# The residual of a fused two-layer trunk: from transposes of x on TensorE to the stored normed x, and a narrow first block

## The chip, the cores and the metric

One core of a Trainium2 chip runs the whole kernel. The metric is device time in microseconds (us) of one launch, the median of three runs. Names of engines: PE is TensorE (PEld its weight loads), DVE is VectorE, ACT is ScalarE, POOL is GpSimd, SP is SyncE, which here only issues DMAs.

## The reference

Two layers over 256 latent and 256 context tokens of width 2048, all in float32. Layer 0 mixes tokens by neighbourhood attention, layer 1 by a state-space scan. Cut to what the change touches:

```python
mod = silu(c) @ ada_w + ada_b                 # shift, scale, gate for the latent tokens
mod_c = silu(c_ctx) @ ada_w + ada_b           # the same for the context tokens
h  = rms_norm(x, norm_w)   * (1 + scale)   + shift
hc = rms_norm(ctx, norm_w) * (1 + scale_c) + shift_c
y, yc = mixer(h, hc)                          # q, k, v, z = h @ w_in; 16 heads; (o * silu(z)) @ w_out
x   = x   + gate   * y                        # the residual of the output projection
ctx = ctx + gate_c * yc
```

Here rms_norm(x, w) is x divided by the root of its mean square (plus 1e-6), times w. The output is rms_norm(x, final_norm_w) after both layers.

## The kernel before

Everything is kept turned: features on the 128 partitions, the 512 tokens (256 latent, 256 context) in the free dimension, so a full activation is 16 feature tiles k of 128x512. A float32 product is made of three matmuls on rounded halves (hi*hi, lo*hi, hi*lo). One weight tile of 128 output columns is 1 MB, is split by ACT into w_hi (line 353) and by DVE into w_lo (line 357), and costs 48 matmuls in `project` (lines 373, 375, 377). Each engine's program is written out by hand, in order, with semaphores between engines. The parts that matter here:

**The first stage** (to 152 us). x is loaded, turned on PE (line 1963) and multiplied by one over its root mean square, which stands as a row repeated on all partitions in PSUM bank 3 (DVE, line 1303); the result is `xn_t`, 16 tiles. The modulation weights na_ada_w (shift and scale: 32 loads of 1 MB, n = 0 to 31) stream through four buffers. SP issues load n when `s_ada_used` says that load n-4 has been multiplied (`mod_products`, line 1995). `BLOCKS` lists which feature tiles are done together, as (first tile, number of tiles): the columns of a block must all be multiplied before any of its tiles has its scale and shift. A block of four tiles takes eight loads, in pieces of 2 KB, a block of two takes four loads, in pieces of 1 KB. When a block's loads are done, ACT copies the row sums (line 821), PE turns them into columns (`mod_columns`, line 2008), DVE adds the biases (lines 1312, 1316), and ACT, DVE and POOL make h (ACT line 796, DVE lines 1323 and 1345, POOL line 630). `first_tiles(c, p)` (lines 2022 to 2024) then multiplies half of a feature tile of block c by three of six weight tiles of the first heads, nine matmuls in one call; the six sums stay in six banks. Those weights come in eight loads of 0.79 MB (`load_first_weights`, line 421); `AHEAD` and `BEHIND` say in which block each stands. The order of `mod_products` and `first_tiles` on PE is the list at the end of the stage in the code.

**The first heads.** `first_heads` on ACT and DVE takes q, k, v, z of heads 0 and 1 from the banks (ACT lines 909 to 915), while `load_head` on SP brings the next weight tiles. Beside the heads the rest of na_ada_w and later ssd_ada_w (gate, and layer 1's modulation) is summed without PE: eight parts l = 0 to 7 in each head, each loaded by POOL (`load_ada`, line 605) into one of two buffers when DVE and ACT have read part l-2, multiplied by DVE (`ada_part`, lines 1409 and 1415) and ACT (`products`, line 858), and added by POOL (`add_products`, line 620).

**The output projection** (912 to 1076 us). 16 tiles of w_out. Behind the matmuls of tile m DVE computes x_t[m] = bank * gate + x_old (line 1555). x_old comes from x and ctx in DRAM: SP loads 128 columns of all tokens in two DMAs (line 471, pieces of 512 B), PE turns them by four transposes (`residual`, line 2169, called at k = 8 of each tile), ACT copies the bank to x_old (lines 968 and 1001). ACT then squares x_t[m] (line 971) and POOL adds the squares (line 693).

The arena is one SBUF buffer that the stages share by offsets. `xn_t` occupies 72 to 104 KB of it, and from the first head on q, k, v, the probabilities, the bias and the sums `ada_acc` and `ada_prod` lie in the same place.

## Time and profile before

| | us |
|---|---|
| median of 3 runs | 2076.57 (2076.32 to 2077.63) |
| the profiled execution, whole | 2077.76 |
| its span | 2075.9 |
| PE busy | 2017.7 |
| DVE busy | 1459.5 |
| ACT busy | 967.6 |
| POOL busy | 665.7 |

The span runs from the first to the last instruction of the profiled execution; its whole time is 1.9 us more. Busy time counts what an engine executes; PE's matmuls overlap, so a mean duration of 363 to 370 ns stands beside a step of 0.23 us from one to the next. The share of a DMA row is the mean busy share of 16 DMA engines, and PEclk 1.00 is the full TensorE clock, 0.50 half of it.

### The profile page before, as it was taken

What the parts mean: (1) busy time and instruction counts of PE and PEld (TensorE: products, weight loads), DVE (VectorE), ACT (ScalarE), POOL (GpSimd) and SP (SyncE); (2) the same over time, 40 slices, a digit from 0 to 9 for tenths busy, and PEclk for the clock granted to TensorE, in tenths of its full rate; (3) what the DMA queues carried; (4) which work ended last, traced back from release to release, by engine and by line L of the source; (5) the groups of instructions that cost most, each with busy time, mean ns of one, the idle gap of its engine ahead of it and who ended that gap; (6) DMA issues with size and microseconds to landing.
All of it is one profiled execution on the core that took longest, in us unless ns stands there. A gap on an engine that the chain in (4) does not pass through costs nothing.

```text
span 2075.9 us, 31012 instructions
## 1 busy us (share of the span) xinstructions
PE 2017.7 (97%) x10458; PEld 1674.5 (81%) x10458; DVE 1459.5 (70%) x2076; ACT 967.6 (47%) x1398; POOL 665.7 (32%) x568
## 2 busy tenths in 40 slices
PE   5998999999999999999999999999999999999998
PEld 3567888888888888878878888888888888888886
DVE  5248777777777777774348877787878787777544
ACT  3244444455444544453355445445444544456443
POOL 1035666556565655635200111111112111110011
PEclk7999999999999999999999999999999999999999
DMA  9996667666666666656353554554554645556654
GB/s 352 338 261 140 168 177 184 174 173 168 172 174 178 178 171 173 164 141 172 102 152 98 149 147 125 144 147 125 143 149 114 167 116 147 138 148 199 226 184 153
DMA packets 422706, 349.23 MB, mean 168 GB/s; under 512 B 13600, under 2 KB 366464, under 8 KB 422016
## 3 DMA queue, kind: packets, MB, share of 16 engines
q1 hardware_dynamic: 397552, 273.43, 46.0%
q0 software_dynamic: 19968, 70.26, 14.1%
q10 hardware_dynamic: 5136, 4.89, 0.7%
q8 instruction: 28, 0.46, 0.1%
q14 instruction: 22, 0.18, 0.0%
HBM read 344.21 MB, written 4.33 MB: 168 GB/s over the span
## 4 chain that ended last, share of the span: by engine, by line
PE 82%; DVE 7%; DMA 4%; ACT 3%; issue 3%; POOL 1%; SPq 0%; DVEq 0%; POOLq 0%; ACTq 0%
PE bank L373 21%; PE bank L377 20%; PE bank L375 20%; DMA arena<-in_na_ada_w_dram 3%; PE bank L2303 3%; PE bank L2305 2%; PE bank L2304 2%; DVE w_lo L357 2%; PE bank L2241 1%; DVE arena L1647 1%; PE bank L2222 1%; PE bank L2107 1%; PE bank L1995 1%; PE bank L2022 1%; PE bank L2236 1%
## 5 line engine op out<-in xcount | busy, mean ns | idle before, releaser
L373 PE MATMUL bank<-act_hi,w_hi 128*128 128x512 f32 (+1 forms) x2448 | 906.0, 370 | 11.5 <-DVE w_lo L357 7.0
L377 PE MATMUL bank<-act_hi,w_lo 128*128 128x512 f32 (+1 forms) x2448 | 888.6, 363 | 0.0
L375 PE MATMUL bank<-act_lo,w_hi 128*128 128x512 f32 (+1 forms) x2448 | 888.0, 363 | 0.0
L357 DVE TENSOR_TENSOR w_lo<-arena,w_hi 128x2048 fp32r<-128x2048 f32 x184 | 435.2, 2365 | 210.8 <-ACT w_hi L353 147.9
L373 PEld LDWEIGHTS bank<-act_hi,w_hi 128*128 128x128 f32 x2448 | 462.7, 189 | 97.3 <-issue 14.4
L377 PEld LDWEIGHTS bank<-act_hi,w_lo 128*128 128x128 f32 x2448 | 462.5, 189 | 73.6
L375 PEld LDWEIGHTS bank<-act_lo,w_hi 128*128 128x128 f32 x2448 | 463.2, 189 | 68.8
L620 POOL TENSOR_TENSOR acc<-acc,arena 128x512 f32<-128x512 f32 x224 | 328.5, 1467 | 126.5 <-ACT arena L858 117.2
L353 ACT ACTIVATE w_hi<-arena 128x2048 fp32r<-128x2048 f32 x138 | 263.8, 1911 | 84.5 <-PE bank L2305 78.2
L1415 DVE SCALAR_TENSOR_TENSOR arena<-arena,cond_c 128x512 f32<-128x512 f32 x240 | 249.4, 1039 | 63.9 <-DMA arena<-in_ssd_ada_w_dram 37.6
L858 ACT ACTIVATE arena<-arena,cond_c 128x512 f32<-128x512 f32 x256 | 171.3, 720 | 261.1 <-POOL acc L620 151.0
L1647 DVE SCALAR_TENSOR_TENSOR arena<-arena,convc 128x512 f32<-128x512 f32 (+1 forms) x192 | 154.0, 802 | 105.6 <-ACT arena L1043 92.4
L728 POOL TENSOR_TENSOR arena<-arena 128x1024 f32<-128x1024 f32 x32 | 76.5, 2392 | 469.3 <-ACT arena L1059 439.9
L1059 ACT ACTIVATE arena<-arena 128x1024 f32<-128x1024 f32 x32 | 33.9, 1060 | 206.0 <-DVE arena L1699 206.0
L2303 PE MATMUL bank<-w_hi,act_hi 128*128 128x512 f32 x256 | 101.1, 395 | 1.9 <-DVE w_lo L357 1.9
L2305 PE MATMUL bank<-w_hi,act_lo 128*128 128x512 f32 x256 | 99.8, 390 | 0.0
L2304 PE MATMUL bank<-w_lo,act_hi 128*128 128x512 f32 x256 | 99.7, 389 | 0.0
L717 POOL TENSOR_SCALAR_AFFINE_SELECT arena<-arena 128x256 f32<-128x256 f32 (+1 forms) x32 | 21.9, 717 | 206.5 <-ACT arena L1172 206.5
L901 ACT ACTIVATE w_hi<-arena 128x2048 fp32r<-128x2048 f32 x43 | 82.0, 1908 | 0.0
L605 POOL DMA_DIRECT2D arena<-in_ssd_ada_w_dram x96 | 68.3, 712 | 33.5 <-DVE arena L1415 25.9
L1048 ACT ACTIVATE arena<-arena 128x512 f32<-128x512 f32 (+1 forms) x48 | 28.6, 597 | 101.4 <-DVE arena L1647 101.4
L1072 ACT ACTIVATE arena<-arena 128x256 f32<-128x256 f32 x128 | 54.3, 495 | 24.2 <-POOL arena L717 24.2
(253 smaller groups left out, 2157.8 us busy)
## 6 DMA issues: line engine op xcount, KB each, us to landing
arena<-in_ssd_w_in_dram SPq DMA_DIRECT2D x81, 1024.0 KB, 6.0
arena<-in_na_w_in_dram SPq DMA_DIRECT2D x58, 1024.0 KB, 7.3
arena<-in_ssd_ada_w_dram POOLq DMA_DIRECT2D x96, 512.0 KB, 4.1
arena<-in_na_ada_w_dram SPq DMA_DIRECT2D x64, 512.0 KB, 8.0
arena<-in_ssd_w_out_dram SPq DMA_DIRECT2D x32, 1024.0 KB, 5.1
arena<-in_na_ada_w_dram POOLq DMA_DIRECT2D x32, 512.0 KB, 4.2
arena<-in_na_w_out_dram SPq DMA_DIRECT2D x16, 1024.0 KB, 6.3
arena<-cs_scr SPq DMA_DIRECT2D x64, 256.0 KB, 5.5
```

Source lines behind the costliest of these rows:

```text
L353: nc.scalar.activation(w_hi[:, n0 % 2, :], raw[slot], ACT.Copy).then_inc(s_hi, 1)
L357: nc.vector.tensor_tensor(w_lo[:, n0 % 2, :], raw[slot], w_hi[:, n0 % 2, :].bitcast(F32), ALU.subtract).then_inc(s_lo, 1)
L373: nc.tensor.matmul(out[:, 0:cols], hi[:, w], act_hi3[:, k, 0:cols], start=(k == 0), stop=False)
L375: nc.tensor.matmul(out[:, 0:cols], hi[:, w], act_lo3[:, k, 0:cols], start=False, stop=False)
L377: mm = nc.tensor.matmul(out[:, 0:cols], lo[:, w], act_hi3[:, k, 0:cols], start=False, stop=(k == KT - 1))
L620: nc.gpsimd.tensor_tensor(acc[:, :], acc[:, :], prod[:, h, :], ALU.add).then_inc(s_gp, 1)
L858: m = nc.scalar.activation(prod[:, h, :], ada_buf[l % 2][:, h, :], ACT.Copy, scale=cond_c[:, k, 1:2])
L1415: m = nc.vector.scalar_tensor_tensor(ada_acc, ada_buf[l % 2][:, h, :], cond_c[:, k, 0:1], ada_acc, ALU.mult, ALU.add)
L1647: m = nc.vector.scalar_tensor_tensor(u, xp[:, 0:segs, k:k + LAT], col(48 + 48 * k), u, ALU.mult, ALU.add)
L2303: nc.tensor.matmul(b[:, :], hi, w_hi[:, n % 2, w], start=(k == 0), stop=False)
L2304: nc.tensor.matmul(b[:, :], hi, w_lo[:, n % 2, w], start=False, stop=False)
L2305: mm = nc.tensor.matmul(b[:, :], lo, w_hi[:, n % 2, w], start=False, stop=(k == IT - 1))
```

## The change

- The residual no longer turns x. After the load of weight tile 6 SP writes `xn_t` to DRAM (`xn_scr`, four DMAs of 1 MB). In the output projection SP loads tile m of it in one DMA of 256 KB, DVE multiplies it by `std_row` (128x512), the root mean square of each token, and uses the product as x_old. The transposes on PE and the copies on ACT are gone.
- `std_row` comes from bank 3: ACT copies it in block 0 to `std_first`, DVE takes the reciprocal, ACT copies that to its place behind the last block.
- What overwrites `xn_t` now waits for the four stores (`s_xsp` 64): on ACT `products(1)` and with it q, k, v of the first head; on POOL `load_bias`; on DVE `ada_part(0)` stands behind z's gate. `ada_part(2)` and `(3)`, `products(3)` and `load_ada(4)` and `(5)` stand earlier in the first heads than before. `load_ada(0)` and `(1)` of the gate stand behind POOL's last piece of h, no longer before its last two.
- `load_x` waits until DVE has made the tile before in the same buffer (`s_free`), no longer for the transposes. POOL's first clearing of `sq_sum`, which lies at another place, waits for the last head.
- `BLOCKS` becomes 2, 4, 4, 4, 2 tiles in place of 4, 4, 4, 2, 2, with `AHEAD`, `BEHIND` and PE's order changed to fit.

What stands in a row on SP at the first stage's begin, before and after. Line 432 (435 in the changed kernel) loads na_ada_w in two DMAs for each n, line 421 (424) the first heads' weights.

```order
L415 DMA plain<-in_ctx_dram 128x2048
L432 DMA arena<-in_na_ada_w_dram 128x2x512 x8
L421 DMA arena<-in_na_w_in_dram 128x2x256 x2
L421 DMA arena<-in_na_w_in_dram 128x2x128 x2
L432 DMA arena<-in_na_ada_w_dram 128x2x512 [waits ada_used]
```

```order
L418 DMA plain<-in_ctx_dram 128x2048
L435 DMA arena<-in_na_ada_w_dram 128x4x256 x4
L424 DMA arena<-in_na_w_in_dram 128x2x256 x2
L424 DMA arena<-in_na_w_in_dram 128x2x128 x2
L435 DMA arena<-in_na_ada_w_dram 128x4x256 x4
L435 DMA arena<-in_na_ada_w_dram 128x2x512 [waits ada_used]
```

The first weights moved ahead of loads 2 and 3; loads 0 to 3 have half as long pieces and are all of block 0.

The end of the same stage on SP:

```order
L432 DMA arena<-in_na_ada_w_dram 128x4x256
L421 DMA arena<-in_na_w_in_dram 128x2x256 [waits first_w_lo_ready]
L421 DMA arena<-in_na_w_in_dram 128x2x256
L421 DMA arena<-in_na_w_in_dram 128x2x128 x2
L449 DMA arena<-in_na_w_in_dram 128x16x128 [waits ada_used] x2
```

```order
L435 DMA arena<-in_na_ada_w_dram 128x4x256
L424 DMA arena<-in_na_w_in_dram 128x2x256 [waits first_w_lo_ready]
L424 DMA arena<-in_na_w_in_dram 128x2x256
L424 DMA arena<-in_na_w_in_dram 128x2x128 x2
L452 DMA arena<-in_na_w_in_dram 128x16x128 [waits ada_used]
L457 DMA xn_scr<-arena 128x2048 [waits x_normed]
L457 DMA xn_scr<-arena 128x2048 x3
L452 DMA arena<-in_na_w_in_dram 128x16x128 [waits ada_used]
```

The four stores stand between the loads of weight tiles 6 and 7.

DVE in the first heads, from the last w_lo of the first stage on (1409 and 1415 are parts of the sums, 1422 and 1428 in the changed kernel; 1459 and 1472 make q_lo; 1361 and 1374 begin the softmax):

```order
L357 TENSOR_TENSOR w_lo<-arena,w_hi 128x2048
L1409 TENSOR_SCALAR arena<-arena,cond_c 128x512
L1415 SCALAR_TENSOR_TENSOR arena<-arena,cond_c 128x512
L1459 SCALAR_TENSOR_TENSOR rounded<-bank,rounded 128x512
L1465 TENSOR_TENSOR rounded<-bank,rounded 128x512
L1498 SCALAR_TENSOR_TENSOR arena<-arena,bank 128x512
L1415 SCALAR_TENSOR_TENSOR arena<-arena,cond_c 128x512 x2
L1459 SCALAR_TENSOR_TENSOR rounded<-bank,rounded 128x512
L1465 TENSOR_TENSOR rounded<-bank,rounded 128x512
L1361 TENSOR_TENSOR bank<-bank,arena 128x256 x2
L1366 TENSOR_REDUCE small<-bank 128x1 x2
L1368 TENSOR_REDUCE small<-bank 128x2
```

```order
L360 TENSOR_TENSOR w_lo<-arena,w_hi 128x2048
L1472 SCALAR_TENSOR_TENSOR rounded<-bank,rounded 128x512
L1478 TENSOR_TENSOR rounded<-bank,rounded 128x512
L1510 SCALAR_TENSOR_TENSOR arena<-arena,bank 128x512
L1422 TENSOR_SCALAR arena<-arena,cond_c 128x512
L1428 SCALAR_TENSOR_TENSOR arena<-arena,cond_c 128x512 x3
L1472 SCALAR_TENSOR_TENSOR rounded<-bank,rounded 128x512
L1478 TENSOR_TENSOR rounded<-bank,rounded 128x512
L1374 TENSOR_TENSOR bank<-bank,arena 128x256 x2
L1379 TENSOR_REDUCE small<-bank 128x1 x2
L1381 TENSOR_REDUCE small<-bank 128x2
L1428 SCALAR_TENSOR_TENSOR arena<-arena,cond_c 128x512 x2
```

Part 0 moved from before q_lo to behind z's gate, part 2 from behind the softmax and the next w_lo to right behind the maxima.

The diff, cut to its core:

```diff
 PRE_AT = (0, 2, 4, 5, 1, 3)
-BLOCKS = ((0, 4), (4, 4), (8, 4), (12, 2), (14, 2))
+BLOCKS = ((0, 2), (2, 4), (6, 4), (10, 4), (14, 2))
 FIRST_K = [k0 for k0, _ in BLOCKS]
-ADA_USED = [2 * k0 if nk == 4 else 24 + 2 * (k0 - 12) for k0, nk in BLOCKS] + [32]
-AHEAD = (0, 2, 4, 6, None)
-BEHIND = (1, 3, 5, None, 7)
+ADA_USED = list(itertools.accumulate([0] + [2 * nk for _, nk in BLOCKS]))
+AHEAD = (0, 1, 3, 5, None)
+BEHIND = (None, 2, 4, 6, 7)
 N_OUT_A = 4 * HEADS
...
-        x_st = [region(16 + 2 * s, 4, P) for s in range(2)]
+        x_st = [region(16 + 2 * s, TOK) for s in range(2)]
+        std_first, std_row = region(70, TOK), region(28, TOK)
         gate_part = region(30, P)
-        x_old, sq_a = region(22, TOK), region(20, TOK)
+        sq_a = region(20, TOK)
         w_third = [region(kb, D, of=rounded) for kb in (40, 48)]
...
-        sq_sum = region(28, TOK)
+        sq_sum = region(22, TOK)
         w_c = [region(kb, D, of=rounded) for kb in (32, 40)]
...
-            load_head(Turn(), (2, 3))
+            load_head(Turn(), (2,))
+            sp.wait_ge(s_xn0, KT)
+            for k in range(0, KT, 4):
+                sp.dma_start(xn_scr[:, k:k + 4, :], xn_t[:, k:k + 4, :]).then_inc(s_xsp, 16)
+            load_head(Turn(), (3,))
             with sp.Fori(2, HEADS) as i:
...
                 if i is not None:
-                    sp.wait_ge(s_xt, i * 2 + (u - 1))
+                    sp.wait_ge(s_free[u], i * 1 + 2 * HEADS)
                 elif u == 0:
                     sp.wait_ge(s_s, HEADS)
+                    sp.wait_ge(s_xsp, 64)
                 apart()
                 m = u if i is None else i * 2 + u
-                for t, src in ((0, x2), (2, ctx2)):
-                    sp.dma_start(x_st[u][:, t:t + 2, :],
-                                 src.rearrange("(t p) d -> p t d", p=P)[:, :, bass.ds(m * P, P)])\
-                      .then_inc(s_xst[u], 16)
+                src = xn_scr[:, m, :] if i is None else \
+                    xn_scr[:, bass.ds(m, 1), :].rearrange("p a t -> p (a t)")
+                sp.dma_start(x_st[u], src).then_inc(s_xst[u], 16)
...
                     pool.wait_ge(s_mod, FIRST_K.index(k) + 1)
-                if k == KT - 2:
-                    load_ada(0, None, True)
-                    load_ada(1, None, True)
                 if k >= 3:
...
+            load_ada(0, None, True)
+            load_ada(1, None, True)
             pool.wait_ge(s_h, KT)
+            pool.wait_ge(s_xsp, 64)
             load_bias(None)
...
             add_products(2, None)
+            load_ada(4, None, True)
             load_bias(1)
-            load_ada(4, None, True)
             add_products(3, None)
+            load_ada(5, None, True)
             mask_bias(1)
-            load_ada(5, None, True)
             for l in range(4, 7):
...
             pool.wait_ge(s_lo, N_OUT_A)
+            pool.wait_ge(s_o, HEADS)
             nc.gpsimd.memset(sq_sum, 0.0).then_inc(s_acc, 1)
...
                     first_hi(AHEAD[c])
+                if c == 0:
+                    act.wait_ge(s_xn0, KT)
+                    nc.scalar.activation(std_first, bank[3][:, :], ACT.Copy)
                 act.wait_ge(s_ada_used, ADA_USED[c + 1])
...
                     first_hi(BEHIND[c])
+            step(nc.scalar.activation(std_row, std_first, ACT.Copy))
+            step.wait()
...
                 act.wait_ge(s_h, KT)
-                for l in range(2):
-                    products(l, Turn())
+                products(0, Turn())
+                act.wait_ge(s_xsp, 64)
+                products(1, Turn())
                 act.wait_ge(s_pre, 1)
...
                 exp_scores(Turn())
+                products(3, Turn())
                 turned_probs(Turn())
...
                 next_hi(4, Turn(base=4))
-                for l in range(3, 8):
+                for l in range(4, 8):
                     products(l, Turn())
...
                     split_hi(act, n + 1, t2, (u + 1) % 2, landed(n + 1, t2))
-                act.wait_ge(s_xt, t2.at(u + 1))
-                nc.scalar.activation(x_old, bank[4 + u][:, :], ACT.Copy).then_inc(s_xo, 1)
                 act.wait_ge(s_free[u], t2.half(n // 2 + 1))
...
             act.wait_ge(s_raw[1], landed(n, Turn()))
-            act.wait_ge(s_xt, KT)
-            nc.scalar.activation(x_old, bank[5][:, :], ACT.Copy).then_inc(s_xo, 1)
             act.wait_ge(s_used, n - 1)
...
                     first_lo(BEHIND[c])
+                if c == 0:
+                    nc.vector.reciprocal(std_first, std_first)
...
                 split_lo(dve, 6, none, 0)
-                ada_part(0, none)
                 query_low(bank[4], none)
...
                 nc.vector.scalar_tensor_tensor(z_g, z_th, 1.0, bank[7][:, :], ALU.add, ALU.mult).then_inc(s_free[1], 1)
+                ada_part(0, none)
                 ada_part(1, none)
...
                 softmax(none)
+                ada_part(2, none)
                 split_lo(dve, 7, none, 1)
...
                 v_low(none)
-                ada_part(2, none)
+                ada_part(3, none)
                 probs_low(none)
                 split_lo(dve, 8, none, 0)
-                for l in range(3, 6):
+                for l in range(4, 6):
                     ada_part(l, none)
...
                     split_lo(dve, n + 1, t2, (u + 1) % 2)
+                dve.wait_ge(s_xst[u], 16 if i is None else i * 16 + 16)
+                nc.vector.tensor_tensor(x_st[u], x_st[u], std_row, ALU.mult).then_inc(s_xo, 1)
                 dve.wait_ge(s_used, t2.at(n + 1))
...
                         dst, bank[u][:, cols], mod_a[:, 2, s, u:u + 1] if i is None else mod_a[:, 2, s, m],
-                        x_old[:, cols], ALU.mult, ALU.add)
+                        x_st[u][:, cols], ALU.mult, ALU.add)
                 mm.then_inc(s_free[u], 1)
...
-            for q in range(8):
-                mod_products(0, q)
-                if q == 2:
-                    norm_rows()
+            mod_products(0, 0)
+            mod_products(0, 1)
+            norm_rows()
+            mod_products(0, 2)
+            mod_products(0, 3)
             mod_columns(0)
-            for c in (1, 2):
+            first_tiles(0, 0)
+            first_tiles(0, 1)
+            mod_products(1, 0)
+            mod_products(1, 1)
+            first_tiles(0, 2)
+            for q in range(2, 8):
+                mod_products(1, q)
+            mod_columns(1)
+            first_tiles(0, 3)
+            for c in (2, 3):
                 for q in (0, 2, 4, 6):
...
                 first_tiles(c - 1, 7)
-            for q in range(2):
-                first_tiles(2, 2 * q)
-                first_tiles(2, 2 * q + 1)
-            mod_products(3, 0)
-            mod_products(3, 1)
-            for p in range(4, 6):
-                first_tiles(2, p)
-            mod_products(3, 2)
-            mod_products(3, 3)
-            first_tiles(2, 6)
-            mod_columns(3)
-            first_tiles(2, 7)
+            for p in range(3):
+                first_tiles(3, p)
             mod_products(4, 0)
             mod_products(4, 1)
-            first_tiles(3, 0)
+            for p in range(3, 5):
+                first_tiles(3, p)
             mod_products(4, 2)
             mod_products(4, 3)
-            first_tiles(3, 1)
+            first_tiles(3, 5)
             mod_columns(4)
-            for p in range(2, 4):
+            for p in range(6, 8):
                 first_tiles(3, p)
...
-            def residual(u, t2, i):
-                pe.wait_ge(s_xst[u], 32 if i is None else i * 32 + 32)
-                if i is not None:
-                    pe.wait_ge(s_xo, t2.at(u - 1))
-                for t in range(4):
-                    mm = nc.tensor.transpose(bank[4 + u][:, t * P:(t + 1) * P], x_st[u][:, t, :], ident[:, :])
-                mm.then_inc(s_xt, 1)
-
             for u in range(2):
-                residual(u, Turn(), None)
                 project(pe, N_OUT_A + u, Turn(), parts=o_ready, ks=range(KT - 1, KT))
...
                 for u in range(2):
-                    project(pe, N_OUT_A + u, t2, parts=lambda k, u=u: residual(u, t2, i) if k == 8 else None,
-                            tile=first if u == 0 else None)
+                    project(pe, N_OUT_A + u, t2, tile=first if u == 0 else None)
...
             with pe.Fori(2, 5) as i:
```

## Rows read from the trace of the kernel before

**Rows 1.** The page: PE's busy time, and the chain that ended last by engine.
```profile
PE 2017.7 (97%) x10458; PEld 1674.5 (81%) x10458; DVE 1459.5 (70%) x2076; ACT 967.6 (47%) x1398; POOL 665.7 (32%) x568
PE 82%; DVE 7%; DMA 4%; ACT 3%; issue 3%; POOL 1%; SPq 0%; DVEq 0%; POOLq 0%; ACTq 0%
```

**Rows 2.** Windows, output projection, PE alone: length, busy (count), PEclk, DMA share, GB/s.
```profile
940.00:1060.00 120.00, 120.00 (x557) 1.00 0.47 128
```

**Rows 3.** Chain of work in the output projection: start, length, what.
```profile
1036.06 0.44 PE bank L2169 x4
1036.50 0.23 PE bank L373
```

**Rows 4.** Timeline of DVE, output projection: start, length, instruction, idle before.
```profile
1042.33 0.88 DVE L1555 SCALAR_TENSOR_TENSOR arena<-bank,mod_a,arena 128x256 f32 x2 [3.27 <-PE bank L377]
...
1077.02 0.69 DVE L1586 TENSOR_TENSOR arena<-arena 128x512 f32<-128x512 f32 x1
```

**Rows 5.** Timeline of PE, first block.
```profile
33.69 1.94 PE L1995 MATMUL bank<-arena 128*32 128x512 f32 x8 [4.24 <-DMA arena<-in_na_ada_w_dram]
...
44.48 1.87 PE L2008 MATMUL bank<-sel_mod,arena 128*128 128x4 f32 x8 [0.72 <-ACT arena L821]
49.03 0.79 PE L2022 MATMUL bank<-act_hi,w_hi 128*128 128x512 f32 x1 [2.68 <-DVE act_lo L1345]
```

**Rows 6.** Timeline of DVE, normalising x.
```profile
28.56 8.88 DVE L1303 TENSOR_TENSOR arena<-bank,arena 128x2048 f32<-128x2048 f32 x4 [4.11 <-issue]
```

**Rows 7.** Timeline of SP: the first loads of na_ada_w behind block 1's first products.
```profile
56.59 1.91 SPq L432 DMA_DIRECT2D arena<-in_na_ada_w_dram  x4
```

**Rows 8.** Windows, first stage: length; PE, PEld, DVE, ACT, POOL busy; PEclk, DMA share, GB/s.
```profile
44.00:54.00 10.00, 6.83 (x20) 5.70 (x21) 6.39 (x15) 5.85 (x10) 3.44 (x4) 0.52 1.06 383
54.00:58.00 4.00, 4.00 (x26) 1.94 (x25) 0.27 (x1) 0.00 (x0) 0.00 (x0) 1.00 0.42 110
...
66.00:114.00 48.00, 45.38 (x251) 28.91 (x253) 15.10 (x31) 13.57 (x22) 7.13 (x8) 1.00 1.07 361
...
128.00:142.00 14.00, 11.56 (x84) 8.08 (x76) 4.55 (x12) 6.06 (x8) 4.48 (x6) 1.00 1.05 300
```

**Rows 9.** Timelines of PE, POOL and ACT, end of the first stage.
```profile
134.82 0.50 PE L2008 MATMUL bank<-sel_mod,arena 128*128 128x4 f32 x4
...
142.25 0.66 PE L2022 MATMUL bank<-act_hi,w_hi 128*128 128x512 f32 x1 [2.69 <-DVE w_lo L1328]
...
152.12 0.60 PE L2115 MATMUL bank<-ident,arena 128*128 128x128 f32 x4
...
136.30 1.62 POOL L605 DMA_DIRECT2D arena<-in_na_ada_w_dram  x2 [9.79 <-DVE gain_a L1316]
...
148.91 0.60 ACT L909 ACTIVATE rounded<-bank 128x512 fp32r<-128x512 f32 x1 [4.65 <-PE bank L2024]
```

**Rows 10.** Windows of PE alone: clock behind two long waits.
```profile
142.00:146.00 4.00, 3.75 (x10) 0.57 0.95 47
...
200.00:204.00 4.00, 4.00 (x16) 0.52 0.80 199
```

**Rows 11.** Page, DMA issues (KB, us to landing): POOL's loads, a store; then line 449's loads.
```profile
arena<-in_na_ada_w_dram POOLq DMA_DIRECT2D x32, 512.0 KB, 4.2
...
x_scr<-arena ACTq DMA_DIRECT2D x1, 2048.0 KB, 8.8
...
DMA to landing us min/median/max: 8.7/10.1/11.5
```

**Rows 12.** Timelines of DVE, POOL, ACT and PE, heads 1 and 2.
```profile
153.41 1.53 DVE L1415 SCALAR_TENSOR_TENSOR arena<-arena,cond_c 128x512 f32<-128x512 f32 x2
...
183.60 2.66 POOL L620 TENSOR_TENSOR acc<-acc,arena 128x512 f32<-128x512 f32 x2 [1.65 <-ACT arena L858]
...
190.21 1.34 ACT L858 ACTIVATE arena<-arena,cond_c 128x512 f32<-128x512 f32 x2 [3.49 <-DMA arena<-in_na_ada_w_dram]
...
199.13 1.97 PE L2092 MATMUL bank<-ident,arena 128*128 128x128 f32 x8 [5.54 <-DVE arena L1379]
```

More of the change, by code:

```diff
@@ L15 @@
+import itertools
 from contextlib import ExitStack, contextmanager
```

3 lines of the change are left out of this document (2 added, 1 removed).

## The prediction

> **What bounds the kernel now.** I read the page first: PE is busy for 2017.7 of 2075.9 us and takes 82% of the chain that ended last [rows 1]. So what is saved on another engine counts only where PE waits for it, and what is saved on PE counts whole where nothing else holds it. Second, the windows of the output projection: in 120 us PE has no idle time, the clock is full and the DMA engines are half used [rows 2]. There PE alone sets the pace. Third, the first stage. DMA runs at 383 GB/s from 44 to 54 us, while PE is busy for 6.8 of these 10; then it falls to 110 GB/s for 4 us, because nothing had been issued until 56.59; from 66 to 114 it is full again at 361 GB/s, and PE is busy for 45.4 of 48 us [rows 7, 8]. So DMA and PE are nearly level in this stage, with DMA the slower, and time that the DMA engines idle there comes back as a wait. Last, the early heads: PE waits once for 5.54 us, at 199.13, and comes back at half clock [rows 10, 12].
>
> **The output projection.** It loses 16 times four transposes. The chain shows them at 0.44 us for four, beside 0.23 us for a matmul [rows 3]. 16 x 0.44 = 7.0 us, all on the path [rows 2]. ACT loses its 16 copies, DVE gains 16 products of 128x512 in SBUF; the nearest row is 0.69 us [rows 4]. They stand before the wait for PE, where DVE idles 3.3 us in a tile [rows 4], and cost nothing; if that cover were gone, each would cost up to 0.7 us, 11 in all. The load of x needs the evacuation of the tile two before instead of its transposes, half a tile (5.5 us) later, and SP's next w_out load stands behind it. It is then issued some 13 us before ACT splits it, and 1 MB loads landed in 8.7 to 11.5 us while the queue was full [rows 11], so it stays hidden. POOL's clearing waits for the last head; POOL is busy for a third of the span [rows 1] and has nothing else to do between the last head and the first square: nothing. **Term: -7.0 us**, from 0 (another engine takes the pace) to -7.4.
>
> **The start.** Block 0 needs four loads in place of eight. They have landed by about 33 us, when the fifth of before had (33.69) [rows 5], so the block waits for the normalised x: DVE starts that at 28.56 and needs 8.9 us [rows 6]. The norm's matmuls stand one load earlier, about 1 us, so 36.5. Then the copy for `std_first` (0.6, as ACT's copy of a bank at 148.91, rows 9), the row copy (0.6 with its start), two columns (half of 1.87 at half clock), and 2.7 us to h [rows 5]: first tile at 41.5, where it was 49.03. That is 7.5 us earlier. DVE's reciprocal of 128x512 costs 0.7 us at the rate of rows 4; DVE is busy for 15 of 48 us in such blocks [rows 8], and nothing waits for it. The rate of a wide reciprocal is in no row here. The Trainium skill (VectorE: DVE Perf Modes, walkthrough of the 8-slice pipeline) says that a reciprocal repeats its divide eight times; by that it would be an estimated 5 us, and the sum would be the same, as DVE's idle time holds that too.
>
> **What the start costs later.** Load 8 can be issued only when `mod_products(1, 0)` is done, and PE reaches that behind 18 matmuls of block 0. PE comes from a wait at half clock (0.52 in 44 to 54, rows 8): ten matmuls at 0.43 us and eight at 0.23 are 6.2 us, the product 1.0, so 48.8. Issued until then are x (4.2 MB), the small inputs (0.3), 8 loads (8.4) and two sets of first weights (1.6): 14.5 MB. Before, 19.5 MB (12 loads, three sets) were through at 54.0. The 5.0 MB less are 13 us at 383 GB/s, so the queue is empty at 41 to 43. It runs again 1.7 us behind an issue (56.59 to about 58, rows 7, 8), at 50.5. DMA idles some 8 us there, in place of 4 us at 54 to 58 [rows 8].
>
> From 50.5 on 24 loads and six sets of weights are left, 29.9 MB, at 361 GB/s 82.8 us: through at 133.3. The same sum for before, 24.9 MB from 58, gives 127, and 130 with its two later gaps. So the debt is about 3 us. PE through the rest: load 27 has four loads and two sets behind it, 5.8 MB or 16 us, and lands at about 118; product 1.0, half a tile of block 2 2.3, column to h 3.6 (4.55 at half clock less half of 1.87, rows 5): 124.8. Then 54 matmuls and four products, 16.5 us: the last column at 141.3, where it was 134.82 [rows 9]. From there to the last block's first tile were 7.4 us, 1.6 of them POOL's two DMA issues ahead of its h [rows 9], which the change moves behind it: 5.9, so 147.2 for 142.25. The last 36 matmuls took 9.9 us until 152.12, since PE came from 2.7 us of waiting at clock 0.57 [rows 9, 10]; at full clock 8.3. The wait is now 1.7 us and I can't tell which clock it leaves: 155.5 or 157.1. **Term: +4 us** (155.5 less 152.1 is 3.4, the other 5.0). Bounds: with the early rate of 383 GB/s all through (78.1 us for 82.8) the debt is gone and the term 0; with 300 GB/s, as at 128 to 142 [rows 8], for the last third of the bytes (10 MB, 5.6 us more) it is about +8.
>
> **The stores.** They are issued behind weight tile 6, whose load waits for the product at about 132. That tile landed 8.7 us behind its issue [rows 11], so 140.8. 4.2 MB at 361 GB/s are 11.6 us; by the kernel's one store of such a size (2 MB in 8.8 us, rows 11) 17.6. They end at 152.4 or 158.4. ACT wants them 3.2 us before PE's end (148.91 of 152.12, rows 9), at 152.9, with 1.4 us of `products(1)` between. Three copies at 0.65 us a step bring q, k and v to 150.9 before, 1.2 us ahead of PE at 152.12 [rows 9]. So at 152.4 nothing is lost (152.4 + 1.4 - 152.9 is 0.9); at 158.4 it is 5.7 us. Queued behind ACT's wait are q, k, v, z and w_hi of tile 7; behind POOL's wait the bias, which needs 6 to 7 us and is due at the softmax, 5.7 us behind PE's end. **Term: +1.5 us**, nearer to the first, as the stores have pieces of 8 KB and the 2 MB store has 1 KB. The Trainium skill (DMA: Bandwidth & Descriptors, anatomy of one DMA) gives about 2 us plus the bytes at 436 GB/s, for GpSimd's queue. By that the estimate is 11.6 us, and 6.8 for the 2 MB store, whose row says 8.8: the measurement is slower than the rule, which is why I don't take zero.
>
> **The first heads.** DVE now has part 0 (1.5 us as [rows 12]) and part 2 (1.5) between z and head 1's probabilities, and exp waits on ACT for part 2's load, which POOL can issue only behind part 0. I work out 0.3 to 1 us for PE's next turn. **Term: +0.7**, 0 to 3. In exchange the parts run ahead. Before, the last products stood at 190.21 behind 3.49 us of waiting for load 7; z's tanh follows them on ACT at 191.45, and 7.7 us later, at 199.13, PE may go on [rows 12]. PE was ready at 193.6. Now `ada_part(3)` and `products(3)` stand before the turned probabilities. Chained by POOL's 2.7 us an add [rows 12] and 4.2 us a load [rows 11], load 5 is issued near 168.5, load 6 at 177, load 7 at 180.6, and products(7) start at 185.5 (times as if the stage before had not moved). Probabilities are then ready at 194.5, for PE at 194.0: 0.5 us of wait in place of 5.54, and no half clock, which cost 2 us of the next 4 [rows 10]. **Term: -6.5**, 0 to -7.6.
>
> **Sum.** -7.0 + 4 + 1.5 + 0.7 - 6.5 = -7.3 us. The profiled execution took 2077.76 (span 2075.9), the median is 2076.57, 1.2 less; I take the difference from the median: 2069.3 us.
>
> **Rivals.**
> A. The early start holds: DMA runs faster than 361 GB/s with so few gaps, and the 7.5 us of block 0 stay. For it: 383 GB/s early, and PE idle only 2.6 of 48 us at 66 to 114. Against: the same rows have the DMA full in that time. -7.0 - 7.5 + 0.7 - 6.5 = -20: 2056.
> B. The second head's wait stays, because load 7 still comes late (it stands on six adds and four loads in a chain, and each late one shifts the rest). -7.0 + 4 + 1.5 + 0.7 = -0.8: 2075.8.
> C. Slower. The stores are the wait: they go at the 2 MB store's rate and share the engines with POOL's 1 MB of gate loads (2.9 us), end at 161, and q comes 8.6 us late for PE; the bias loads, which moved 47 GB/s with all engines occupied [rows 10] while PE was in the first stage, now stand in the first head and hold POOL's chain, so the later wait stays. -7.0 + 5 + 8.6 + 0.7 = +7: 2084. It decides if the stores end over 8 us behind PE's need (beyond 161).
> D. The output projection keeps its time, since a tile's evacuation with DVE's product becomes the bound: -7.3 + 7.0: 2076.
>
> **Chances.** Forecast 0.62 (its own range 2065 to 2073.5), A 0.10, B 0.14, C 0.10, D 0.04. What can be told from no change here is 0.2%, 4.2 us: faster takes the forecast and A, 0.72; B and D are the same, 0.17 with a small rest; C is slower, 0.11. The range of 2061 to 2078 leaves out A and C.
>
> **What would show it.** The first tile on PE at 41 to 42; GB/s near zero for some us before 50; the turn of v (the first PE work behind the stage) at 155 to 158 in place of 152.12; the stores landing near 152; no wait over 2 us on PE near 200; a tile of the output projection in 10.9 us and PE without idle time there. I am wrong in the front if DMA doesn't run dry at 43, and in the heads if PE's wait for the second head's probabilities (line 2092) stays above 3 us.

## The result, and the profile after

| | us (median of runs) |
|---|---|
| before, same chip | 2077.84 (2076.32 to 2080.68, 6 runs) |
| changed | 2086.31 (2083.77 to 2088.65, 6 runs) |
| ratio changed / before | 1.004 (95%: 1.003 to 1.0051) |

The change makes the kernel 8.5 us slower here, and 6.5 us slower in a second series (r12 below). The forecast was 2069.3, and the range ended at 2078: it was wrong in sign. The profiled execution of after is its slowest, 2088.65 us with a span of 2087.0, so it stands 11.1 us behind the span of 2075.9 before. Page of the changed kernel, answering to [rows 1]:

```profile
PE 2015.1 (97%) x10394; PEld 1673.3 (80%) x10394; DVE 1492.3 (72%) x2093; ACT 957.0 (46%) x1384; POOL 693.2 (33%) x568
PE 52%; DMA 12%; DVE 11%; issue 11%; POOL 7%; ACT 6%; POOLq 0%; DVEq 0%; ACTq 0%; SPq 0%
```

PE has 2.6 us less to do, but it is only half of the chain that ended last, where it was 82%. That half belongs to this execution and not to the change: the page of r12, the same kernel, says 82% again, and r8, which is faster than before, has 51%. What these two executions share is told under r12.

The first stage, PE and then windows (columns as in [rows 8]), for [rows 5, 8, 9]. Line 2011 is now `mod_products`, 2024 `mod_columns`, 2038 the first matmul of `first_tiles`:

```profile
41.22 0.80 PE L2038 MATMUL bank<-act_hi,w_hi 128*128 128x512 f32 x1 [2.67 <-DVE act_lo L1356]
...
57.86 1.94 PE L2011 MATMUL bank<-arena 128*32 128x512 f32 x8 [1.59 <-DMA arena<-in_na_ada_w_dram]
60.74 1.93 PE L2011 MATMUL bank<-arena 128*32 128x512 f32 x8 [0.94 <-DMA arena<-in_na_ada_w_dram]
64.17 1.93 PE L2011 MATMUL bank<-arena 128*32 128x512 f32 x8 [1.50 <-DMA arena<-in_na_ada_w_dram]
...
121.38 1.07 PE L2011 MATMUL bank<-arena 128*32 128x512 f32 x8 [1.03 <-DMA arena<-in_na_ada_w_dram]
...
144.75 0.50 PE L2024 MATMUL bank<-sel_mod,arena 128*128 128x4 f32 x4
...
151.34 0.47 PE L2038 MATMUL bank<-act_hi,w_hi 128*128 128x512 f32 x1 [1.85 <-DVE w_lo L1339]
```

```profile
44.00:50.00 6.00, 6.00 (x29) 3.61 (x27) 3.24 (x2) 1.48 (x1) 0.00 (x0) 0.72 0.01 3
...
58.00:74.00 16.00, 12.85 (x45) 6.50 (x44) 4.29 (x14) 5.20 (x10) 3.57 (x4) 0.50 1.06 379
...
78.00:80.00 2.00, 2.00 (x18) 0.64 (x11) 0.00 (x0) 0.00 (x0) 0.00 (x0) 1.00 0.15 26
```

The first tile comes at 41.22, as forecast, and the DMA is dry from 44 to 50 (3 GB/s). When it runs again, PE takes each load as it lands, with waits between, and from 58 to 74 it has half the clock (0.50, the 1.2 GHz level). The last column ends up at 144.75 for 134.82 [rows 9]. (r12 has it at 143.49, after a first tile at 39.79: one execution of this kernel differs from another by over a microsecond here.)

The end of the stage and the first head: SP, POOL, ACT, then PE, for [rows 9, 12]. Line 457 issues the stores, 612 the gate's loads, 647 the bias, 871 is `products`, 923 takes q; on PE 2132 turns v, 2109 turns the probabilities:

```profile
136.16 5.48 SPq L457 DMA_DIRECT2D xn_scr<-arena  x4
...
147.19 1.61 POOL L612 DMA_DIRECT2D arena<-in_na_ada_w_dram  x2
153.93 1.33 POOL L647 DMA_DIRECT2D arena<-in_na_rpb_dram  x2 [5.13 <-DMA xn_scr<-arena]
...
159.52 1.33 ACT L871 ACTIVATE arena<-arena,cond_c 128x512 f32<-128x512 f32 x2 [7.65 <-DMA arena<-in_na_ada_w_dram]
161.31 1.34 ACT L871 ACTIVATE arena<-arena,cond_c 128x512 f32<-128x512 f32 x2 [0.46 <-DMA arena<-in_na_ada_w_dram]
162.55 0.57 ACT L923 ACTIVATE rounded<-bank 128x512 fp32r<-128x512 f32 x1
```

```profile
164.15 1.12 PE L2132 MATMUL bank<-ident,arena 128*128 128x128 f32 x4 [4.38 <-ACT arena L927]
183.61 1.79 PE L2109 MATMUL bank<-ident,arena 128*128 128x128 f32 x8 [3.01 <-DVE arena L1392]
...
213.81 1.09 PE L2109 MATMUL bank<-ident,arena 128*128 128x128 f32 x8 [0.55 <-DVE arena L1392]
```

Read the first block from the bottom. q (162.55) stands behind two pairs of gate products on ACT, and these wait for POOL's loads issued from 147.19 on, which land at 159.5 and 161.3. That is 12.2 and 13.1 us for 0.5 MB each, where the page of before has 4.2 as the median [rows 11] and 5.3 to 5.7 for these two. The stores themselves were through at 153.9 at the latest (POOL goes on there), 6 us before PE's last first tile ended. So the wait for the stores, which I had priced, costs nothing, and the loads that share the engines with them cost 4.38 us on PE.

The 11.1 us, read from the start of the same instruction in both traces ("turned probabilities" is PE's transposition of them, line 2092 before and 2109 now):

| PE reaches | before | after | later by |
|---|---|---|---|
| end of first tiles | 152.12 | 159.77 | 7.6 |
| turn of v | 152.12 | 164.15 | 12.0 |
| turned probabilities, head 0 | 165.61 | 183.61 | 18.0 |
| the same, head 1 | 199.13 | 213.81 | 14.7 |
| the same, head 3 and on | 301.82 | 314.81 | 13.0 |
| the same, last head | 897.65 | 914.50 | 16.9 |
| span's end | 2075.9 | 2087.0 | 11.1 |

### The profile page after: what moved, and what is told of

Read it like the earlier page. It is cut to its first block, busy times and chain, and to the rows that moved or that the text cites. A ratio compares the mean times of both kernels' runs of the same rounds, so it can differ in the third digit from the quotient of the medians.

```text
span 2087.0 us, 30856 instructions
## 1 busy us (share of the span) xinstructions
PE 2015.1 (97%) x10394; PEld 1673.3 (80%) x10394; DVE 1492.3 (72%) x2093; ACT 957.0 (46%) x1384; POOL 693.2 (33%) x568
## 3 DMA queue, kind: packets, MB, share of 16 engines
q0 software_dynamic: 19968, 70.26, 13.5%
## 4 chain that ended last, share of the span: by engine, by line
PE 52%; DMA 12%; DVE 11%; issue 11%; POOL 7%; ACT 6%; POOLq 0%; DVEq 0%; ACTq 0%; SPq 0%
PE bank L376 12%; PE bank L380 12%; PE bank L378 12%; DMA arena<-in_ssd_ada_w_dram 7%; POOL acc L627 4%; DMA arena<-in_na_ada_w_dram 4%; ACT arena L871 3%; PE bank L2310 3%; PE bank L2312 2%; PE bank L2311 2%; DVE arena L1428 2%; DVE w_lo L360 2%; POOL acc L621 2%; PE bank L2248 1%; DVE arena L1663 1%
## 5 line engine op out<-in xcount | busy, mean ns | idle before, releaser
L360 DVE TENSOR_TENSOR w_lo<-arena,w_hi 128x2048 fp32r<-128x2048 f32 x184 | 443.9, 2412 | 193.3 <-ACT w_hi L356 150.3
L627 POOL TENSOR_TENSOR acc<-acc,arena 128x512 f32<-128x512 f32 x224 | 335.9, 1499 | 136.3 <-ACT arena L871 127.1
```

Source lines behind the costliest of these rows:

```text
L360: nc.vector.tensor_tensor(w_lo[:, n0 % 2, :], raw[slot], w_hi[:, n0 % 2, :].bitcast(F32), ALU.subtract).then_inc(s_lo, 1)
L627: nc.gpsimd.tensor_tensor(acc[:, :], acc[:, :], prod[:, h, :], ALU.add).then_inc(s_gp, 1)
```

## The experiments

The ratios are to runs of the kernel before in the same series, "r1" and so on name the kernels. The change stands at 2086.31 in its own series and at 2083.91 in r12's, 2084.6 over all eleven executions, which lie between 2082.89 and 2088.65. So where a variant of the change is set beside it, a difference of 2 to 3 us or less can't be told from none, and the traces have to speak.

**r1, the residual alone** (with PE's order of before for these blocks).
```
-BLOCKS = ((0, 2), (2, 4), (6, 4), (10, 4), (14, 2))
+BLOCKS = ((0, 4), (4, 4), (8, 4), (12, 2), (14, 2))
-AHEAD = (0, 1, 3, 5, None)
-BEHIND = (None, 2, 4, 6, 7)
+AHEAD = (0, 2, 4, 6, None)
+BEHIND = (1, 3, 5, None, 7)
```


> The changed kernel with the blocks of before put back (4, 4, 4, 2, 2 columns, with their loads and their order on TensorE); the residual from the stored normed tokens stays. Theory A (the narrow first block runs the DMA dry at 44 to 50 us and makes all that follows late, the gate's first loads above all; the residual's part is a gain): the stage of the first tiles ends at 152 to 153 us as before, the out projection is 6 us shorter, the waits of the first heads stay under 4 us in all: 2070 to 2075 us. Theory B (it is the stores of 4 MB and the order of the first heads that cost): the turn of v still comes 5 us or more behind the last first tile, and the time is over 2080.

2074.73 us, ratio 0.9986 (0.9977 to 0.9995).

**r2, the blocks alone**, the kernel before with the new table and PE's new order:

> The kernel before with nothing but the new blocks (2, 4, 4, 4, 2), their loads and their order on TensorE. Theory A: the first stage ends at 158 to 160 us instead of 152.1, the DMA is dry from 44 to 50 us, and the second head's wait near 200 us stays: 2082 to 2087 us, as slow as the full change or slower. Theory B: the front costs little, 2076 to 2080.

2086.95 us, ratio 1.0047 (1.0034 to 1.0061). So the blocks alone cost 9.3 us, and the residual alone wins 2.9. The two add up to 6.4 us, beside the 8.5 and 6.5 of the change. PE in r1:

```profile
151.58 0.66 PE L2131 MATMUL bank<-ident,arena 128*128 128x128 f32 x4 [2.14 <-ACT arena L927]
170.76 1.97 PE L2108 MATMUL bank<-ident,arena 128*128 128x128 f32 x8 [5.50 <-DVE arena L1392]
...
200.93 1.09 PE L2108 MATMUL bank<-ident,arena 128*128 128x128 f32 x8
```

The time is in theory A's range, but its "waits under 4 us in all" fails: the first head still waits 7.6 us. And the stage of the first tiles ends at 149.4, not at 152 to 153, mostly by the clock. The last 36 matmuls stand behind a wait of 1.85 us in r1 and took 8.4 us at full clock; r6 has the same blocks and the same wait, was granted 0.61 over the next 4 us, and needs 9.9. r2 has the last column at 142.47 and no wait at the turn of v (159.76) or at the first probabilities (173.26): 7.6 us later than before at both. Its second head waits 5.10 us, where before waited 5.54.

**r3, two products ahead of the first tiles.**
```
+            mod_products(1, 0)
+            mod_products(1, 1)
             first_tiles(0, 0)
             first_tiles(0, 1)
-            mod_products(1, 0)
-            mod_products(1, 1)
```


> The changed kernel with the second block's first two groups of modulation products ahead of the first tiles on TensorE, instead of behind two of them. Theory A: the loads behind them are issued at about 40 us instead of 49.5, the DMA does not run dry, TensorE does not wait at 55 to 66 us and keeps its full clock there; the last column comes at 138 to 140 us instead of 144.9, the stage ends 4 to 6 us earlier, and the time is 2079 to 2082 us. Rival: the transfers are only moved, another gap takes the place of this one, and less than 2 us are won (2085).

2080.51 us, ratio 1.002 (1.0011 to 1.0029): 5.8 us less than the change in its first series, 3.4 less than in r12's.

```profile
44.00:50.00 6.00, 6.00 (x34) 4.01 (x37) 3.05 (x2) 1.49 (x1) 0.00 (x0) 1.00 0.80 294
...
56.31 1.71 PE L2011 MATMUL bank<-arena 128*32 128x512 f32 x8 [3.99 <-DMA arena<-in_na_ada_w_dram]
59.03 1.94 PE L2011 MATMUL bank<-arena 128*32 128x512 f32 x8 [1.01 <-DMA arena<-in_na_ada_w_dram]
...
138.55 0.50 PE L2024 MATMUL bank<-sel_mod,arena 128*128 128x4 f32 x4
```

The dry stretch holds 294 GB/s now, and the last column is 6.2 us earlier. TensorE still waits for two loads (5.0 us), which A had denied, while the DMA moves 341 to 394 GB/s (56 to 68 us). And the last column is still 3.7 us later than before: filling the dry stretch wins back 6.2 of the 9.9 us by which the change is late there (144.75 for 134.82).

**r4, copies of q, k, v ahead of the gate's products on ACT.**
```
-                products(0, Turn())
                 act.wait_ge(s_xsp, 64)
-                products(1, Turn())
...
+                products(0, Turn())
+                products(1, Turn())
```


> The changed kernel with ScalarE's copies of the first head's q, k and v and its tanh ahead of the first two pairs of gate products, behind the wait for the stores. If q waits for the gate's first loads (landed at 159.5 and 161.3 us): the turn of v is no longer later than the last first tile by more than 2 us, 2.5 to 4 us are won there, and some 2.5 at the end (2083 to 2084). Rival: the chain of gate products, then 3 us later, sets the first head's probabilities or the second head, and nothing is won (2086).

2084.38 us, ratio 1.0032 (1.002 to 1.0044), between the two series of the change. The turn of v follows the last first tile without a wait (159.48). The first probabilities then wait 6.74 us:

```profile
179.87 1.97 PE L2109 MATMUL bank<-ident,arena 128*128 128x128 f32 x8 [6.74 <-DVE arena L1392]
...
210.44 1.09 PE L2109 MATMUL bank<-ident,arena 128*128 128x128 f32 x8 [0.85 <-DVE arena L1392]
```

4.7 us at the turn of v become 3.7 at the first head's probabilities, and 0.9 at head 2's (264.05 for 264.90): PE then waits 2.08 us for w_lo (at 237.95), for 1.18 in the change. So the first half of the expectation holds and the gain at the end does not; the rival was right that the chain of gate products takes it back.

**r5, the stores early**, ahead of the ninth load of the modulation (and no longer behind weight tile 6).
```
+                    for k in {8: (0, 4, 8, 12)}.get(n, ()):
+                        sp.wait_ge(s_xn0, KT)
+                        sp.dma_start(xn_scr[:, k:k + 4, :], xn_t[:, k:k + 4, :]).then_inc(s_xsp, 16)
                     if n >= 4:
                         sp.wait_ge(s_ada_used, n - 3)
```


> The changed kernel with the four stores of the normed tokens issued ahead of the ninth group of modulation weights (at about 39 us, into the stretch where the DMA is dry) instead of at 136 us. Theory A (the stores share the DMA with the gate's first loads and hold TensorE's first head): the gate's loads land within 7 us of their issue instead of 12 to 13, q does not wait for them, and the turn of v follows the last first tile within 1 us; the stores last some 10 us, of which 6 to 7 fill the dry stretch, so the last column is 0 to 3 us later: 2080 to 2084 us. Rival C (the stores are harmless, the wait comes from the late last column alone): the gate's loads still take over 10 us, 2086 to 2089.

2082.82 us, ratio 1.0027 (1.0016 to 1.0038): 3.5 us less than the change in its first series, 1.1 less than in r12's, so the time decides little. The 44 to 50 window moves 426 GB/s. POOL, ACT and PE:

```profile
148.57 1.61 POOL L612 DMA_DIRECT2D arena<-in_na_ada_w_dram  x2
...
153.26 2.63 ACT L871 ACTIVATE arena<-arena,cond_c 128x512 f32<-128x512 f32 x4
...
162.59 0.60 PE L2132 MATMUL bank<-ident,arena 128*128 128x128 f32 x4
```

The loads land 4.6 and 5.0 us behind their issue; ACT takes the gate's products and waits for neither. So the stores' share of the DMA was what made these loads late: the "harmless" of this expectation's rival C is refuted. The last column is 1.4 us later (146.13), as A had it, and the last 36 matmuls ran at half clock here (0.57 over their first 4 us), at full clock in the change. So the turn of v is only 1.6 us earlier, and of the 2.8 us at the first probabilities 0.7 are left at head 2's (264.21).

**r6, r1 with the first head's order of before** (r4's edit, and on DVE):
```
                 softmax(none)
-                ada_part(2, none)
                 split_lo(dve, 7, none, 1)
                 normalise(none)
                 v_low(none)
-                ada_part(3, none)
+                ada_part(2, none)
                 probs_low(none)
```


> The blocks of before with the stored residual (2074.7 us), and in the first head the order of before again: ScalarE's copies ahead of the first gate products, VectorE's third and fourth part behind the copy of v and the low half of the probabilities. In that kernel TensorE waited 2.14 us at the turn of v and 5.50 us at the first turned probabilities, at half clock behind it. Theory A (the order of the first head and the late gate loads cost together): the first wait goes, the second is under 3 us; but the second head's wait comes back in part, since part 2 and the fourth load are later: 2071 to 2074. Rival: the wait only moves to the second head, as the kernel before had it there (5.5 us), 2074 to 2077.

2075.35 us, ratio 0.9989 (0.998 to 0.9998): no gain over r1. The first probabilities are 1.6 us earlier than in r1 (169.13), those of the second head, behind a wait of 4.91, 2.7 later (203.62 for 200.93). The rival holds: a part taken out of the first head is missing in the second.

**r7, the change without DVE's product.** It leaves out the scaling of the normed x back to x.
```
-                nc.vector.tensor_tensor(x_st[u], x_st[u], std_row, ALU.mult).then_inc(s_xo, 1)
+                dve.sem_inc(s_xo, 1)
```


> The changed kernel without VectorE's product of the stored tokens with the factor in the out projection (the residual added there is the normed tokens, not scaled back: this part of the computation is left out). The product's price on TensorE's path is read off: TensorE waited 0.38 us at 932.1 and 1.29 us at 944.5 for VectorE. Theory A: 1 to 1.7 us, 2084.5 to 2085.5. Rival: 16 products by 0.68 to 1.79 us hold VectorE, and the port they share with GpSimd makes more of it: over 3 us, 2083 or less.

2085.27 us, ratio 1.0041 (1.0028 to 1.0055): 1.0 less than the change in its first series, 1.4 more than in r12's. The time shows no price of the sixteen products, and speaks against the rival's 3 us. In the trace the wait at the projection's third tile goes from 1.29 to 0.48, 0.8 us; the rest of that projection is alike.

**r8, r6 with two of the four stores early**, one ahead of load 12 of the modulation and one ahead of load 28:

> The kernel of r6 with one store ahead of the 13th group of modulation weights (about 47 us), one ahead of the 29th (about 106 us), and only two at 128 us. Theory A: each store of 1 MB costs 2.5 us of DMA, the first two fall into stretches where it had room (56 to 60 and 112 to 116 us); the gate's loads land by 144 us and the bias is there 5 us earlier; another 1 to 3 us against r6: 2069 to 2073. Rival: the DMA is the bound from 60 to 112 us, and the first store makes the stage 2.5 us later: as r6 or slower.

2073.1 us, ratio 0.9979 (0.997 to 0.9988). It is 2.3 under r6, with intervals that overlap. The first head waits 1.89 us for r6's 3.32, the second 5.68 for 4.91:

```profile
201.53 1.97 PE L2109 MATMUL bank<-ident,arena 128*128 128x128 f32 x8 [5.68 <-DVE arena L1394]
```

**r9, r1 with four stores spread**, and DVE's first part ahead of the copies again:
```
+                    for k in {12: (0,), 18: (4,), 24: (8,), 28: (12,)}.get(n, ()):
+                        sp.wait_ge(s_xn0, KT)
+                        sp.dma_start(xn_scr[:, k:k + 4, :], xn_t[:, k:k + 4, :]).then_inc(s_xsp, 16)
...
                 split_lo(dve, 6, none, 0)
+                ada_part(0, none)
                 query_low(bank[4], none)
```


> The blocks of before, the stored residual, and its four stores ahead of the 13th, 19th, 25th and 29th group of modulation weights; VectorE's first part ahead of the copies of q and k again, its third part ahead of the normalisation as in the change. Theory A (late gate loads behind the stores, and parts that VectorE then does between softmax and normalisation, are what the residual's part paid in the first head): the gate's first loads land within 6 us of 137, the turn of v comes at 152, the first turned probabilities at 168 or before (170.8 in the kernel with the late stores), the second head has no wait over 1 us; with the out projection 2069 to 2072 us. Rival: four early stores take 10 us of DMA in a stretch that is bound by it, the last column is 3 us or more later: 2073 to 2077.

2072.44 us, ratio 0.9979 (0.997 to 0.9988).

```profile
168.33 1.09 PE L2108 MATMUL bank<-ident,arena 128*128 128x128 f32 x8 [1.65 <-DVE arena L1392]
197.00 1.09 PE L2108 MATMUL bank<-ident,arena 128*128 128x128 f32 x8 [0.70 <-DVE arena L1392]
```

Both waits are small at last. The time is just over theory A's 2069 to 2072. The rival has its part: there are four waits for loads between 69 and 135, where before had two, and the last column is 138.18 for 134.82, 3.4 later. r9 changes two things, the stores' place and part 0's, and no run separates them. A wait that before did not have is left: 2.31 us for w_lo at 224.75, with DVE's w_lo behind ACT's w_hi, and that behind gate products which waited 3.19 us for POOL's add. r8, r9 and r10 can't be told apart in time; they are the fastest, some 4 to 5 us (0.2%) under before and 11 to 14 under the change.

**r10, r9 with tile 1's product beside tile 0's:**

> The same, with the product for the out projection's second tile done beside that of the first, ahead of the sums of the gate, instead of between the gate's first part and the evacuation of the tile. Theory: the evacuation of tile 1 is 0.7 to 1.1 us earlier, TensorE's wait of 1.3 to 1.7 us at tile 3 shrinks to 0.5, and the time is 1 us less than without it, at the edge of what these runs can tell. Rival: the load of tile 3 sets that wait, no difference.

2072.56 us, ratio 0.9975 (0.9965 to 0.9985). The wait at the third tile shrinks as expected, 1.66 to 0.48. The medians are 0.1 us apart and can't show a microsecond, and between the two profiles the first stage differs by 3.6 us in its end, 1.6 of them by the clock behind the same wait of 1.85 us. Inconclusive in time, clear in the trace.

**r11, the new blocks with everything mended** (r3's and r9's edits on the change):

> The new blocks (2, 4, 4, 4, 2) with the two groups of products ahead of the first tiles, and the stores and VectorE's first part as in the two kernels before this. Theory A (first tiles 8 us earlier buy nothing, since the stage is bound by the loads to 112 us and TensorE does the same work): 2 to 5 us slower than the same with the blocks of before, 2073 to 2076. Rival (the new blocks are a gain once nothing holds them): as fast or faster, 2070 or less.

2075.54 us, ratio 0.999 (0.9978 to 1.0003), 3.1 more than r9. A holds, though the intervals of r9 and r11 overlap: the first tile is 6.4 us earlier (42.07 for 48.50), the turn of v 6.2 us later (159.20 for 153.03). PE waits for loads six times between 56 and 121.

**r12, the change again:**

> The changed kernel again, with nothing altered. In its profiled execution (2088.65 us, its slowest) the chain of gate products ran 4 us later within each head than in that without the product, and TensorE lost 3.9 us more at the end of the heads. If that belongs to single executions: a profile without it (last turned probabilities 14.6 us behind the last turn of v, not 18.4) or a time near 2084 to 2085 beside others near 2088. If it belongs to the kernel: 18.4 us again.

2083.91 us (2082.89 to 2087.67), ratio 1.0035 (1.0021 to 1.0049). PE's waits in the last head, first the change, then this run:

```profile
900.94 0.47 PE L376 MATMUL bank<-act_hi,w_hi 128*128 128x512 f32 x1 [2.17 <-DVE act_lo L1534]
...
908.15 0.50 PE L376 MATMUL bank<-act_hi,w_hi 128*128 128x512 f32 x1 [1.91 <-DVE act_lo L1534]
```

```profile
903.58 0.50 PE L376 MATMUL bank<-act_hi,w_hi 128*128 128x512 f32 x1 [1.43 <-DVE act_lo L1534]
```

The 3.9 us at the end of the heads belong to single executions: the last probabilities stand 14.6 us behind the last turn of v here, as in before and in ten of the other kernels. The distance was 18.4 in that first profile and 17.3 in r8's. The chain of ACT, POOL and DVE over the gate's products goes with it. In r12 its last products on ACT begin 2.2 us behind the turn of v in heads 2 and 3, as in the first profile; at head 4 they are 1.3 us ahead of it, and from head 5 on 2.4. In the first profile they stay 1.5 to 2.6 us behind to the last head. r7 makes the same step at head 5. So there are two rhythms, and most executions leave the late one after a few heads; what makes them leave it stays open.

## Why the prediction was wrong

Three terms failed: what the start costs later, the stores and, by most, the first heads. By the prediction's terms, in the profiled execution (in brackets: forecast):

- **The start [first tile at 41.5]**: 41.22, and 39.79 in r12. Right, with some luck in the tenths, and so was the DMA's dry stretch [41 to 43, again at 50.5: the 44 to 50 window].
- **What the start costs later [+4, bounds 0 to +8]**: +7.6, and +7.6 in r2 alone. This is the first step that failed, in size. I had summed bytes at 361 GB/s and let PE follow ("load 27 lands at about 118"). PE took it at 121.4, and the last column is late by the same 3.4 us (144.75 for 141.3). Two things were missing. Behind the dry stretch, loads come one by one, and PE, with waits between them, stayed at half clock for 16 us. And the DMA had next to nothing to do again at 78 to 80 (26 GB/s), as SP issues only when PE has freed a slot. How much each of them cost is not shown; r3, which fills the dry stretch, takes 6.2 us off the last column. The clock at the end was the good one of my two cases, by luck: 8.4 us for 36 matmuls behind 1.85 us of waiting, but they began at 151.34 and not 147.2. Behind the same wait six of the profiles have full clock (8.3 to 8.4 us for the 36), and six have 0.57 to 0.67 over the next 4 us (9.9 to 10.0 us).
- **The stores [+1.5, bounds 0 to 5.7]**: the named wait, zero. They were done by 153.9, in the forecast's span [152.4 to 158.4], but PE needed them later, as the stage was late. From the first issue to the last landing they took 17 us here and 16.5 in r5, with other transfers ahead of them in the queue, where the forecast had 11.6 or 17.6. The Trainium skill's rule for GpSimd's queue (DMA: Bandwidth & Descriptors, anatomy of one DMA), about 2 us and the bytes at 436 GB/s, also gave an estimate of 11.6 us. The trace comes near its rate (426 GB/s in r5, 44 to 50) and not its sum. What I had not put into the term: the gate's two loads are issued behind them, while they run. They took 12.2 and 13.1 us for 5.3 to 5.7, and q stood behind them: +4.4 on PE. r4 shows that this was the wait (with q ahead of the products it is gone), r5 that the stores made it. Rival C spoke of these loads, but only as a burden on the stores; it was the other way round.
- **The first heads [+0.7, bounds 0 to 3]**: +6.0, outside the bounds, and the largest miss. I had priced parts 0 and 2 at 1.5 us each and found 0.3 to 1 us of that on PE's path. Between v's turn and the probabilities, before had only part 1 of the gate ahead of the softmax. Now parts 0 and 1 stand there and part 2 in front of the normalisation, and POOL, whose chain started late, adds beside DVE. DVE's rows, before and then after, the softmax from lines 1361 and 1374 on, its scalings at 1376 and 1389:

```profile
156.79 0.76 DVE L1361 TENSOR_TENSOR bank<-bank,arena 128x256 f32<-128x256 f32 x2
...
162.29 0.88 DVE L1376 TENSOR_SCALAR arena<-arena,small 128x512 f32<-128x512 f32 x2
```

```profile
167.16 4.60 DVE L1428 SCALAR_TENSOR_TENSOR arena<-arena,cond_c 128x512 f32<-128x512 f32 x3
...
172.88 0.75 DVE L1374 TENSOR_TENSOR bank<-bank,arena 128x256 f32<-128x256 f32 x2
...
175.47 2.22 DVE L1428 SCALAR_TENSOR_TENSOR arena<-arena,cond_c 128x512 f32<-128x512 f32 x2
...
180.01 3.02 DVE L1389 TENSOR_SCALAR arena<-arena,small 128x512 f32<-128x512 f32 x2
```

  From the turn of v to the softmax there are 8.7 us, where before had 4.7; from there to the two scalings 7.1 for 5.5; and the scalings take 3.02 us for 0.88 beside POOL's adds. PE is held by less than the sum, since DVE had been ahead of it. r9, with part 0 ahead of q and the loads in time, has the 4.7 us again (157.71 behind 153.03) but still 6.9 and 3.16: its first head is 1.8 us longer than before's.
- **The second head's wait [-6.5]**: 0.55 for 5.54 us, as forecast, but from 18.0 to 13.0 late is only -5.0. Among what is missing is a new wait of 1.18 us for w_lo at 240.41, behind the gate's chain in the second head. That the wait near 200 goes is due to the parts done earlier: in r6 and r8, where part 2 is late again, it is back. What the second head won, the first had paid. In r1, without the front, the two heads and what follows come to +2.6 us (last turned probabilities 900.23 for 897.65); I had -4.3.
- **The out projection [-7.0]**: -5.8 from the last probabilities to the end. A tile takes 10.88 us for 11.36 over most of the way, near the 0.44 of [rows 3], but PE waits 0.38 and 1.29 us near the projection's start. There DVE has the sums of the gate to do, tile 1's product stands between, and "cost nothing" was an average of a steady tile. r7 and r10 show 0.8 and 1.2 us of it.
- **The reciprocal**: 3.34 us, hidden. At the rate of a plain pass it would have been 0.7; the Trainium skill (VectorE: DVE Perf Modes, walkthrough of the 8-slice pipeline) had led to an estimate of 5. The measurement lies between, 4.8 times the plain pass.

Sum: 7.6 + 4.4 + 6.0 - 5.0 + 3.9 (that execution alone) - 5.8 = 11.1. Without the 3.9 it is 7.2, between the 8.5 and 6.5 us of the two series.

The result is near rival C's 2084, but by luck: its deciding point (stores beyond 161) was not reached, its later wait did not stay, and the 8.6 us it had for the stores are 4.4, while it had 0.7 for the first heads and nothing for the slow scalings. Right in it was that the stores meet the gate's loads and that POOL's chain is late in the first head. Nor was the late stage the reason for the first heads' cost: in r1, where the stage ends early, the turn of v and the first probabilities are 19.2 us apart, for 13.5 before.

## What to carry to other kernels

A stage whose DMA is level with TensorE gained nothing from an early start here. When a consumer of loads is put behind other work, count when the next load can be issued, and allow for half clock in the stretch where loads come singly (0.50 from 58 to 74). When stores are added, ask which small loads are issued while they run and who stands behind these. Work moved out of a waiting head into the head before is not free there: look at what it stands in front of. And profile the changed kernel twice before a part of its chain is explained: here 3.9 us and the 52% belonged to one execution.

## What the hardware showed beyond that

- Stores of the 4.2 MB in four pieces ran at 426 GB/s (r5, 44 to 50); the loads at that place in the kernel before, at 383 [rows 8].
- Two 0.5 MB loads from POOL's queue, issued into 4 MB of stores from SP's queue, landed after 12.2 and 13.1 us. The same two took 5.3 to 5.7 in the kernel before and 4.6 to 5.0 in r5, where the stores were through.
- DVE's two scalings of 128x512 beside POOL's adds: 3.02 us, and 3.16 in r9; 0.88 where POOL did not add.
- Behind the same wait of 1.85 us PE comes back at full clock (the 2.4 GHz level) in six of the profiles, and in six others at half clock for the first matmuls (0.57 to 0.67 as the mean of 4 us): 8.3 or 9.9 us for the same 36 matmuls. What decides it is open.
- The same program has executions in which a chain of three engines keeps a rhythm 4 us later until the last head, and others that leave it by head 4 or 5: 3.9 us at their end; what decides it is open.
